# A four-layer encoder trunk in fp32 on one NeuronCore: row norms applied after the products, norm gains folded into the weight split, stage borders worked bank by bank, weight slots rotated

## The reference

```
for i in range(2):
    if i == 1:
        kv = rms_norm(h, kv_norm) @ w_kv                 # 1024 x 512, shared k and v
    h = h + 0.5 * (silu(gate) * up) @ w_down             # gate, up = rms_norm(h, g) @ w_gate_up; D_FF 2816
    z = rms_norm(h, mix_norm[i]) @ w_in[i]               # 1024 x 1024
    y_mix = pooling (i == 0) or banded attention with sinks, QK norm and rotary (i == 1)
    y_mem = attention of 4 heads over rms_norm(mem, g) @ w_mem_kv[i]      # 1024 x 512
    h = h + concat(y_mix, y_mem) @ w_out[i]              # 1024 x 1024
    h = h + 0.5 * swiglu(rms_norm(h, ffn2_norm[i]))
rms_norm(x, g) = x * rsqrt(mean(x * x) + 1e-6) * g
```

## Time and profile before

| | us |
|---|---|
| median of 3 runs (981.19 to 987.0) | 981.24 |
| span of the profiled execution | 977.7 |
| TensorE busy | 949.3 (97%) |
| DVE busy | 554.0 (57%) |
| ACT busy | 457.7 (47%) |
| POOL busy | 50.0 (5%) |
| HBM read over the span | 171.28 MB, 176 GB/s |
| mean granted TensorE clock | 0.994 |

### The profile page before, as it was taken

How to read it: one execution, slowest core, us unless ns; L and a number is a source line. 1 busy time by engine, 2 the same in 40 slices (tenths; PEclk the granted TensorE clock), 3 DMA queues, 4 the chain that set the end, 5 groups by cost and what they waited for, 6 DMA issues and landing times.

```text
span 977.7 us, 12400 instructions
## 1 busy us (share of the span) xinstructions
PE 949.3 (97%) x4515; PEld 779.0 (80%) x4515; DVE 554.0 (57%) x650; ACT 457.7 (47%) x642; POOL 50.0 (5%) x85
## 2 busy tenths in 40 slices
PE   7999999999999999999899999999998999999998
PEld 5888888887777888888688888888876878888886
DVE  5655454674557455555676546455776565455552
ACT  6544444444435443444545434353556455353441
POOL 3300000010000000000210000000130000000000
PEclk9999999999999999999999999999999999999999
DMA  9966556364145746464366555652740246646442
GB/s 318 293 220 202 184 183 203 129 237 161 42 150 193 250 149 212 157 214 172 108 215 215 187 199 173 213 169 103 266 129 1 86 164 212 217 152 209 163 129 86
DMA packets 121054, 172.74 MB, mean 177 GB/s; under 512 B 5649, under 2 KB 95921, under 8 KB 121025
## 3 DMA queue, kind: packets, MB, share of 16 engines
q1 hardware_dynamic: 118416, 164.65, 50.6%
q0 software_dynamic: 2464, 7.64, 2.4%
q10 hardware_dynamic: 144, 0.07, 0.0%
HBM read 171.28 MB, written 1.05 MB: 176 GB/s over the span
## 4 chain that ended last, share of the span: by engine, by line
PE 90%; DVE 5%; ACT 2%; DMA 1%; issue 1%; POOL 1%; SPq 0%; POOLq 0%; DVEq 0%; ACTq 0%
PE ps L1042 19%; PE ps L1044 19%; PE ps L1043 19%; PE ps L1114 8%; PE ps L1116 8%; PE ps L1118 8%; PE ps L1097 2%; DVE w_lo L712 2%; PE ps L1034 1%; DMA w_raw<-in_ffn_w_gate_up_dram 1%; DVE mainT_lo L738 1%; ACT squares L489 1%; DVE xn L729 1%; PE ps L1180 1%; PE ps L1216 1%
## 5 line engine op out<-in xcount | busy, mean ns | idle before, releaser
L712 DVE TENSOR_TENSOR w_lo<-w_raw,w_hi 128x1024 fp32r<-128x1024 f32 x308 | 371.0, 1224 | 154.8 <-ACT w_hi L469 147.8
L469 ACT CAST w_hi<-w_raw 128x1024 fp32r<-128x1024 f32 x308 | 317.1, 1052 | 145.5 <-PE ps L1118 71.3
L1042 PE MATMUL ps<-w_hi,mainT_hi 128*128 128x512 f32 x832 | 329.8, 396 | 6.9 <-DVE w_lo L712 3.0
L1044 PE MATMUL ps<-w_hi,mainT_lo 128*128 128x512 f32 x832 | 324.7, 390 | 0.0
L1043 PE MATMUL ps<-w_lo,mainT_hi 128*128 128x512 f32 x832 | 324.1, 390 | 0.0
L1042 PEld LDWEIGHTS ps<-w_hi,mainT_hi 128*128 128x128 f32 x832 | 156.2, 188 | 42.3 <-issue 9.0
L1044 PEld LDWEIGHTS ps<-w_hi,mainT_lo 128*128 128x128 f32 x832 | 156.2, 188 | 33.3
L1043 PEld LDWEIGHTS ps<-w_lo,mainT_hi 128*128 128x128 f32 x832 | 156.4, 188 | 30.9
L505 ACT ACTIVATE silu_g<-ps 128x256 f32<-128x256 f32 x88 | 33.8, 384 | 234.3 <-PE ps L1044 234.1
L745 DVE TENSOR_TENSOR act_f<-ps,silu_g 128x256 f32<-128x256 f32 x88 | 37.3, 424 | 169.6 <-PE ps L1097 128.6
L1114 PE MATMUL ps<-w_hi,actT_hi 128*128 128x512 f32 x352 | 109.3, 392 | 0.3
(11 more groups left out here) (153 smaller groups left out, 530.0 us busy)
## 6 DMA issues: line engine op xcount, KB each, us to landing
w_raw<-in_ffn_w_gate_up_dram SPq DMA_DIRECT2D x176, 512.0 KB, 4.6
w_raw<-in_ffn_w_down_dram SPq DMA_DIRECT2D x88, 512.0 KB, 4.1
w_raw<-in_w_in_dram SPq DMA_DIRECT2D x16, 512.0 KB, 6.2
w_raw<-in_w_out_dram SPq DMA_DIRECT2D x16, 512.0 KB, 5.2
w_raw<-in_w_mem_kv_dram SPq DMA_DIRECT2D x8, 512.0 KB, 4.0
gain<-in_ffn_norm_dram POOLq DMA_DIRECT2D x4, 512.0 KB, 6.3
w_raw<-in_w_kv_dram SPq DMA_DIRECT2D x4, 512.0 KB, 4.0
h<-in_x_dram SPq DMA_DIRECT2D x2, 512.0 KB, 4.2
```

The source lines that it names most:

```text
L469: nc.scalar.copy(half(w_hi[s], b), half(w_raw[s], b)).then_inc(hi_ready[s], 1)
L712: nc.vector.tensor_tensor(half(w_lo[s], b), half(w_raw[s], b), half(w_hi[s], b).bitcast(F32), ALU.subtract).then_inc(lo_ready[s], 1)
L1042: pe.matmul(dst, x_hi, wh, start=start, stop=False)
L1044: return pe.matmul(dst, x_lo, wh, start=False, stop=stop)
```

## The change

- The transposes read h itself (`turn_h`), not xn. `norm_rows` is gone. The row factor is applied where a product leaves PSUM: as a scale in silu (ACT), in the gating (DVE), in `z_copy` (ACT) and `kv_copy` (DVE).
- The nine gains are loaded once, as 72 rows of 128 numbers by five small DMAs on ACT's queue, turned by TensorE and kept as columns `gain_col`. The weight split multiplies by them: ACT makes the hi half by two activations of 512 columns with a pointer scale, DVE the lo half by two scalar_tensor_tensor of 512 columns. Units of w_down and w_out have no gain and keep one instruction for a half.
- h after ffn1 is turned once (H45) for kv and ffn2; the memory's transposes and splits are kept for both layers (M), with its sums of squares behind its splits in ffn0.
- Residuals go bank by bank (512 columns), the last step of an ffn bank by bank (`end_bank`), and the transposes of the new h stand among the last and the next products.
- Loads are halves of a unit in two DMAs each (256 KB) with a wait of their own. A stage takes the slots behind those of the stage before, and the last down unit of an ffn has a slot of gate and up.
- `low_unit` of the next stage's units now stands behind `kv_copy` on DVE at mkv0, kv and mkv1.

```diff
@@ ACT: the weight split
-                    nc.scalar.copy(half(w_hi[s], b), half(w_raw[s], b)).then_inc(hi_ready[s], 1)
+                    if GAIN[stage] is None or j is None:
+                        ins = nc.scalar.copy(half(w_hi[s], b), half(w_raw[s], b))
+                    else:
+                        for kk in (2 * b, 2 * b + 1):
+                            g = GAIN[stage] * KC + 4 * j + kk
+                            ins = nc.scalar.activation(w_hi[s][:, kk, :], w_raw[s][:, kk, :], ACT.Copy,
+                                                       scale=gain_col[:, g:g + 1])
+                    ins.then_inc(hi_ready[s], 1)
...
+            def split_mem():
+                for t in range(NT):
+                    for b in range(2):
+                        split("M", t, b, "side")
+                row_sum("M", 0)
+                row_sum("M", 1)
@@ DVE: the weight split and the gating
+                            ins = nc.vector.scalar_tensor_tensor(
+                                out=w_lo[s][:, kk, :], in0=w_raw[s][:, kk, :], scalar=gain_col[:, g:g + 1],
+                                in1=w_hi[s][:, kk, :].bitcast(F32), op0=ALU.mult, op1=ALU.subtract)
...
-                nc.vector.tensor_tensor(act_f[:, t, :], ps[:, GU_BANK + t, FB:2 * FB], silu_g[:, t, :],
-                                        ALU.mult).then_inc(act_ready, 1)
+                nc.vector.scalar_tensor_tensor(out=act_f[:, t, :], in0=ps[:, GU_BANK + t, FB:2 * FB],
+                                               scalar=row_scale(norm, t), in1=silu_g[:, t, :],
+                                               op0=ALU.mult, op1=ALU.mult).then_inc(act_ready, 1)
@@ DVE: the end of an ffn
+                low(name, UNIT[name, "end"], None)
+                gated(f, last, 1, norm, None)
+                if FOLLOWING[name] is not None:
+                    low_unit(FOLLOWING[name], 0)
...
+                if FOLLOWING[name] is not None:
+                    low_unit(FOLLOWING[name], 1)
+                residual(r, 0.5, 0, 0)
+                residual(r, 0.5, 0, 1)
...
@@ DVE: the order behind ffn1 (mkv0 and mkv1 alike)
-            ffn(1, rope_tables)
-            residual(2, 0.5)
-            norm_rows(4, 0)
-            norm_rows(4, 1)
...
-            proj_low("kv", 2)
-            kv_copy(kv_sb, kv_done, kv_ready, 0, "kv")
...
+            ffn(1, "H3", "H45", rope_tables)
+            kv_copy(kv_sb, kv_done, kv_ready, 0, "kv", "H45")
+            low_unit("ffn2", 0)
+            low_unit("ffn2", 1)
@@ PE: the end of an ffn, and the next product's hook
+                end_bank(0, 0)
+                end_bank(0, 1)
...
+                end_bank(1, 0)
+                turn_h(after, 0, 0)
+                end_bank(1, 1)
+                turn_h(after, 0, 1)
...
+            def late_tile(name):
+
+                def hook(k):
+                    if k == 2:
+                        turn_h(name, 1, 0)
+                    elif k == 4:
+                        turn_h(name, 1, 1)
+                return hook
@@ SP: a load waits for its own half
+            def load(unit, b, parts, turn=0):
+
+                s, c = unit
+                if not isinstance(turn, int) or c + turn > 0:
+                    sp.wait_ge(lo_ready[s], (c + turn) * 2 + (b - 1))
+                for dst, src in parts:
+                    sp.dma_start(dst, src).then_inc(raw_landed[s][b], 16)
```

More of the change, by code:

```diff
@@ L501, in silu, with split @@
+            def split(name, t, b, dest="main"):
+                act.wait_ge(turned[t][b], split_no(name))
+                nc.scalar.copy(tr_hi[dest][:, 4 * b:4 * b + 4, t * P:(t + 1) * P],
+                               ps[:, turn_bank(t, b), :].rearrange("p (k t) -> p k t", k=4)).then_inc(split_hi[t][b], 1)
+            def silu(f, c, t, norm):
+                s, used = UNIT[f"ffn{f}", "gate"][1]
                 if t == 0:
-                    act.wait_ge(gu_done, c + 1)
+                    act.wait_ge(gu_done, f * STEPS + c + 1)
@@ L507, in actT_high @@
+                nc.scalar.activation(silu_g[:, t, :], ps[:, GU_BANK + t, 0:FB], ACT.Silu,
+                                     scale=row_scale(norm, t)).then_inc(silu_ready, 1)
             def actT_high(e):
@@ L685, in _ @@
             attention(1)
[L686 to L694 removed]
+            split_out("ffn3", 1, "H8")
+            ffn(3, "H8", None)
         @block.vector
@@ L1091, in turn_act @@
-                def turn_act(c, split=False):
+                    mm = product(gate, c, t, ps[:, GU_BANK + t, :], "main", norm, first, hook)
+                    if t == 0:
+                        mm.then_inc(gu_done, 1)
+                def turn_act(c, bank):
                     pe.wait_ge(act_ready, (c0 + c) * 2 + 2)
                     for fc in range(2):
-                        bank = TR_BANK + (fc if split else 0)
                         for t in range(NT):
```

913 lines of the change are left out of this document (469 added, 444 removed).

## The result

The change made the kernel slightly slower. The median went from 982.56 us to 989.17 us (16 runs of each), the ratio of the runs is 1.0062 with a 95% interval of 1.0043 to 1.0082. The profiled execution took 987.3 us where that of before took 977.7. I had forecast 978.1 us with a range of 971 to 985.5: the time lies outside the range, and on the other side of no change. It is within 1% all the same, which had the chance of 0.85.

The account below looks back on a forecast made before the run. TensorE, 97% busy, bounds the kernel: only its number of products and transposes and its waits count. Terms summed to -3.15 us: span 977.7 to 974.55, median 3.5 above the span, so 978.1; range 971 to 985.5.

Parts of the forecast that it names:

- The loops: Loop steps: products start 0.227 us apart and nothing waits; dearer DVE and ACT instructions don't matter; no term in the sum.
- Half clock behind the new waits: Rival: half clock behind four waits of 2.4 to 2.5 us (memory, z0, ffn2, z1): 6.8 us more, 984.9; chance 0.15.
- The start: First product near 11.3 us instead of 14.37, -3.0; half clock on products after TensorE's idle stretch, +1.7.
- the rival of the smaller loads: Rival: smaller loads move less, so the start wins nothing: 3.0 us more, 981.1; chance 0.10.
- Second steps: Second step of each ffn: second gate unit later by 0.53 us on top of 0.22, four times, +2.1.
- memory: ffn0: ACT's two sums of squares delay the first down unit, so TensorE waits 2.5 us, +2.5.
- mkv0, kv: Next unit waits behind DVE's copies, 2.4 us each: +1.8 behind mkv0; -6.15 behind kv, where the norm chain goes.
- out0 and out1: Behind out0 and out1: waits of 2.3 us each go, 0.15 more each for transposes in fours, -4.9.
- z1: Behind mkv1 and in z1: DVE's list makes TensorE wait 4.1 us, +4.5; half clock behind that, +1.7.
- The end: Kernel's end: last residual of 512 columns and a last store half as large, -0.8.
- the pointers are free: Rival: pointer operands cost nothing for instructions in a row, so their delays fall away: 974.5; chance 0.15.
- the copies don't hold TensorE: Rival: DVE's copies don't hold TensorE up because units get split earlier: 15.4 us less, 962.7; chance 0.08.

Follow-up runs that it names:

- the fillers: Changed kernel with unneeded TensorE products in its waits before ffn0's first down products, z0, z1 and ffn2: 986.39 us median, ratio 1.0047.

## Why the prediction was wrong, step by step

The sum was -3.15 us and the profiled executions differ by +9.6; 12.75 us are to be explained.

- **The loops (the step that failed first).** "So only two things can move the time: the number of products and transposes on TensorE, and the places where TensorE waits": this left out the pace at which products follow each other. "In the loops neither matters" was said of DVE and ACT, and it holds: no wait came there. But the prediction took the pace, 0.227 us, as untouched, because their number and shapes were. The new tile moved actT off its address: +6.6 us. No term of the sum stood for it, and no rival. The addresses were open to see in the order of the allocations; the price was not in any row of before, where all tiles of these products lie at multiples of 128.
- **Half clock behind the new waits (a rival that came true).** The memory, z0 and ffn2 cost 1.6 us each in this execution, 4.8 in all, and z1 two stretches for the one forecast, +1.5. The rival priced four such stretches at 6.8, and the four measured 6.4. I read the earlier trace rows as if there were one point between 1.5 and 2.7 us of idle, on the one execution that I had, and gave it 0.15 as one event. The runs show no such point: the wait of 1.49 us itself was followed by half clock in 6 of 14 executions, and waits of 2.2 to 2.4 us in 7 of 12. About 0.9 us for each of the three waits that no later wait takes up (memory, z0, ffn2), 2.8 in all, belonged into the sum. Against it, attention of layer 1 had a stretch of half clock in the profile of before and none in that of after, -1.5.
- **The start: -3.0 + 1.7 forecast.** The first product was to come at 11.3 and came at 12.79. TensorE stood 1.07 us for the last of the gain rows to land (the row of L1361 above) before it turned h, which I had at 6.7 to 7.8 without a wait; and the stretch of half clock with products in it was 4.4 us, not 3.4. +1.9 together. The loads themselves were as fast as assumed: the queue moved 383 GB/s over 8 to 14 us in loads of 256 KB, against the 373 of the earlier trace rows, so the rival of the smaller loads is out.
- **Second steps, memory, mkv0, kv: right.** In the second step of an ffn the second gate unit starts 0.90 us behind its forerunner in place of 0.227 (29.21 to 30.11 in ffn0), 0.68 late where 0.75 (0.22 and 0.53) was said; the memory 2.3 between starts for 2.5; from ffn0's last product to z0's first it is 1.9 us more (forecast 1.8); from ffn1's last to ffn2's first 15.05 us for 21.1 (forecast 14.9). That DVE runs its list in order, and the unit therefore stands behind a copy that must wait for the last product, was the right reading of the order, and moving the unit showed it.
- **out0 and out1: right.** No wait is left, and ffn3 and out1 together are 2.2 us shorter when the pace is undone, with 0.6 given back in the second step.
- **z1: the wait was 2.2, not 4.1.** The end of DVE's chain was right; TensorE came there later, since it had lost 1.6 us at half clock behind its wait at z1's start; in the run with the gain columns last, at full clock there, the wait is 3.62. Where a wait is fixed by another engine, what TensorE loses ahead of it costs nothing more. -1.9.
- **The end:** -1.1 for -0.8.

These come to 11.4 of the 12.75 (6.6 + 6.3 - 1.5 + 1.9 - 1.9, with a further 0.4 at a wait in ffn1's second step behind the rope tables, -0.3 at the end and -0.1 in small differences); 1.3 us I can't assign. That the pointers are free and that the copies don't hold TensorE are both excluded by the rows. Without the shifted tile the time would just have come inside the range: the run with the gain columns last has a median of 984.64, 6 us above its middle, and four of its ten runs lie above 985.5. That would have been luck in part, since the half clock was mis-sized all the same. The forecast also put the median 3.5 us above the span; every run on record lies 1.8 above its core's span, and the rest of the 3.5 was that the profiled execution of before, at 977.7, was faster than its median.

## What to carry to other kernels

A change to a kernel's tiles is a change to its addresses: when a new tile goes in, put it behind the ones that TensorE reads, or make it a multiple of 128 bytes a partition (the measurements are of fp32 products of 512 columns alone), and look at the median duration of the products by operand, which shows the slip where no wait does. A wait of TensorE has two prices, its length and the half clock about it: here behind about half of the waits of 1.5 to 2.9 us and behind all unfilled ones of 3.4 and more, at about 1.6 us for a stretch of 3.4 us and up to 3.2 for one of 6.8. Price it so, and where it can't be removed, fill it with products that nobody reads. Ahead of a wait that another engine fixes, neither helps.

## What was not expected of the hardware

- fp32 products of 512 columns with stationary tiles of 128 x 128 started 0.2325 us apart in place of 0.2263 with the stationary operand 32 or 64 bytes off a multiple of 128, and about 7 ns later each with the moving operand 32 bytes off; both off did not add. The duration of one product rose from a median of 389 ns to 395 or 396.
- The same wait of 2.39 us was followed by a granted clock of 0.50 over 3.4 us in one place and of 1.00 in another of the same execution. After the fillers, which are bf16 products of 256 columns, it was 1.00 at all four places.
- Attention of layer 0 had a stretch of half clock (0.50 over 264 to 270) in some profiles and none in others, 6 of 14, always about 2 us behind the same wait of 1.49 us. Why it came in some and not in others was not settled.
